# Expert stages with x parked in HBM, 21 instead of 14 up slabs beside the crossings, low parts behind the batches, and another order at the program's start

## What is computed

```python
def peer_ffn(x, w_q, sub_keys, u, v):
    q = (x @ w_q).reshape(B, S, PEER_HEADS, 2, hq)
    s_half = jnp.einsum('bshpc,hpkc->bshpk', q, sub_keys)
    top_s, top_i = lax.top_k(s_half, PEER_TOPK)
    ...
    best_s, best_pos = lax.top_k(cand_s.reshape(B, S, PEER_HEADS, n_cand), PEER_TOPK)
    experts = jnp.take_along_axis(...)
    gate = jax.nn.softmax(best_s, axis=-1)
    ...
        h = jax.nn.gelu(jnp.einsum('ted,td->te', u[ec], xc))
        return jnp.einsum('te,ted->td', gc * h, v[ec])
```

## Time and profile before

| | |
|---|---|
| runs | 4186.75 us median (4180.42 to 4187.92, 3 runs) |
| profiled execution | 4185.16 us, its span 4183.9 us |
| TensorE busy | 3972.6 us, 95% of the span; weight loads 92% |
| VectorE, ScalarE, GpSimd busy | 66%, 48%, 4% |
| mean granted clock | 0.975 of full speed |
| expert stage 0 | about 2335 to 3179 us; crossings 2574 to 2724 |
| expert stage 1 | about 3324 to 4166 us; crossings 3563 to 3717 |

### The profile page before, as it was taken

One profiled execution on the slowest core, in us unless ns is written; L12 is line 12 of the kernel. 1 busy time (PEld: TensorE's weight loads), 2 busy tenths in 40 slices (PEclk: granted clock), 3 DMA queues, 4 the chain that ended last, 5 costly groups with the idle time before them and its releaser, 6 DMA issues.

```text
span 4183.9 us, 78739 instructions
## 1 busy us (share of the span) xinstructions
PE 3972.6 (95%) x34162; PEld 3844.9 (92%) x34162; DVE 2741.8 (66%) x4076; ACT 1988.6 (48%) x2624; POOL 173.3 (4%) x212
## 2 busy tenths in 40 slices
PE   7989999999998999989989999899999999899999
PEld 7979999899996999979987899899998899899998
DVE  5566665665655657556545799844856699864765
ACT  4445444454443545454425545644444544654443
POOL 0011000110000000010013100000000000000000
PEclk9999999899999999999988999999999999999999
DMA  5534555345454455524541354455754355445754
GB/s 207 194 115 143 197 186 196 112 151 192 167 197 144 169 194 189 184 101 155 196 165 54 128 197 169 147 189 196 257 193 151 132 181 192 143 168 197 250 200 151
DMA packets 118633, 716.61 MB, mean 171 GB/s; under 512 B 13952, under 2 KB 19728, under 8 KB 37008
## 3 DMA queue, kind: packets, MB, share of 16 engines
q1 hardware_dynamic: 90864, 660.64, 44.7%
q10 hardware_dynamic: 26400, 43.28, 3.0%
q0 software_dynamic: 1024, 7.64, 0.5%
HBM read 690.38 MB, written 21.13 MB: 170 GB/s over the span
## 4 chain that ended last, share of the span: by engine, by line
PE 76%; DVE 12%; ACT 7%; issue 2%; DMA 2%; ACTq 1%; SPq 0%; DVEq 0%
PE psum L650 23%; PE psum L652 23%; PE psum L651 23%; DVE slab_low L1894 5%; ACT slab_high L1397 4%; PE psum L1040 1%; PE psum L1376 1%; DVE room L2541 1%; DMA peer_gates<-room 1%; DVE room L2520 1%; DVE h_parts L2177 1%; PE psum L1023 1%; ACT room L1808 1%; PE psum L1053 1%; ACT room L1645 1%
## 5 line engine op out<-in xcount | busy, mean ns | idle before, releaser
L1894 DVE TENSOR_TENSOR slab_low<-slab,slab_high 128x2048 fp32r<-128x2048 f32 x622 | 1424.9, 2291 | 880.9 <-ACT slab_high L1397 878.5
L650 PE MATMUL psum<-h_parts,slab_high 128*128 128x256 f32 x5632 | 1585.2, 281 | 56.5 <-DVE h_parts L2177 46.2
L1397 ACT ACTIVATE slab_high<-slab 128x2048 fp32r<-128x2048 f32 x630 | 1191.5, 1891 | 915.5 <-PE psum L652 798.4
L651 PE MATMUL psum<-h_parts,slab_high 128*128 128x256 f32 x5632 | 1564.2, 278 | 0.0
L652 PE MATMUL psum<-h_parts,slab_low 128*128 128x256 f32 x5632 | 1563.7, 278 | 0.0
L650 PEld LDWEIGHTS psum<-h_parts,slab_high 128*128 128x128 f32 x5632 | 1071.3, 190 | 78.0 <-issue 49.3
L650 PE MATMUL psum<-hidden_parts,slab_high 128*128 128x256 f32 x3840 | 1068.3, 278 | 26.5 <-DVE hidden_parts L2549 11.3
L651 PEld LDWEIGHTS psum<-h_parts,slab_high 128*128 128x128 f32 x5632 | 1071.8, 190 | 2.6 <-issue 2.4
L652 PEld LDWEIGHTS psum<-h_parts,slab_low 128*128 128x128 f32 x5632 | 1070.5, 190 | 0.0
L651 PE MATMUL psum<-hidden_parts,slab_high 128*128 128x256 f32 x3840 | 1062.0, 277 | 0.0
L652 PE MATMUL psum<-hidden_parts,slab_low 128*128 128x256 f32 x3840 | 1061.9, 277 | 0.0
(11 more groups left out here) (324 smaller groups left out, 3332.5 us busy)
## 6 DMA issues: line engine op xcount, KB each, us to landing
slab<-in_up SPq DMA_DIRECT2D x176, 1024.0 KB, 4.8
slab<-in_keys_up SPq DMA_DIRECT2D x128, 1024.0 KB, 4.8
slab<-in_keys_down SPq DMA_DIRECT2D x128, 1024.0 KB, 4.8
slab<-in_down SPq DMA_DIRECT2D x88, 1024.0 KB, 4.8
slab<-in_w_in SPq DMA_DIRECT2D x16, 1024.0 KB, 4.7
slab<-in_wq SPq DMA_DIRECT2D x16, 1024.0 KB, 4.8
peer_gates<-room ACTq DMA_DIRECT2D x64, 256.0 KB, 2.3
room<-peer_gates ACTq DMA_DIRECT2D x64, 256.0 KB, 4.6
```

The source lines that it names most:

```text
L650: nc.tensor.matmul(out, lhs[0], rhs[0], start=first, stop=False, **options)
L651: nc.tensor.matmul(out, lhs[0], rhs[1], start=False, stop=False, **options)
L1397: nc.scalar.activation(k.high[m % PARTS][:, 0:width], k.slabs[m % RING][:, 0:width], ACT.Copy).then_inc(k.rounded.up())
L1894: nc.vector.tensor_tensor(k.low[m % RING][:, 0:width], k.slabs[m % RING][:, 0:width], k.high[m % PARTS][:, 0:width], ALU.subtract).then_in ...
```

## The change

It does five things.

- **Room for hidden values.** The constants are sorted so that six (`LASTING`) come first. The others, and x, now lie at the bottom of the room. All stages but peer carve above them (`FLOOR`). peer carves its hidden rows from the very bottom: 32 + 21 up slabs fit.
- **x in HBM.** GpSimd stores x to `parked_x` after the squares, ScalarE waits for that before the first up is activated, and GpSimd loads x back once the 61st pair of hidden rows is split (`v.above_x` = 61); VectorE waits for it before the final adds.
- **EXTRA = 21.** The 32 batches lie in 38 windows, s = 2 to 39, beside 21 up slabs; then 11 downs alternate with the last 11 ups, 21 downs go beside the second multiplications, 32 behind. The number of slabs, matmuls, one-hots and gate transfers stays.
- **Low parts behind the batches.** In the crossings VectorE's `rest_slab` stands behind the step's batches.
- **Start and end.** Vectors load ahead of x, the constants wait until slab 1 is in. ScalarE and VectorE do six h chunks before slab 1; TensorE's second slab lags by 6 chunks (`FIRST_LAG`); the squares come last. x is stored in four pieces.

The diff, without the hunks that only move views above `FLOOR`:

```diff
--- before.py
+++ after.py
@@ -41,7 +41,7 @@
 NSEL = PH * TOPK
 ROUNDS = NKEYS // 2
 HALF = ROUNDS // 2
-EXTRA = 14
+EXTRA = 21
 BATCH = 8
 BATCHES = T // BATCH
 RETURNS = 6
@@ -106,13 +106,17 @@
     return {k: np.asarray(v, np.float32) for k, v in c.items()}
 
 
+LASTING = ("ident", "ones", "causal", "iota", "pick", "npick")
 CONST = constants()
+CONST = {k: CONST[k] for k in LASTING + tuple(k for k in CONST if k not in LASTING)}
 CONST_AT = {}
 _at = 0
 for _k, _v in CONST.items():
     CONST_AT[_k] = (_at, _v.shape[1], _v.shape[0])
     _at += _v.shape[1]
 CONST_W = _at
+LASTING_W = sum(CONST[k].shape[1] for k in LASTING)
+FLOOR = CONST_W - LASTING_W + DC * T
 
 
 VECTORS = [(f"ffn1_norm{l}", 8) for l in range(2)] + [(f"mix_norm{l}", 8) for l in range(2)] \
@@ -131,7 +135,7 @@
 
 RING = 4
 PARTS = 3
-AHEAD = 2
+FIRST_LAG = 6
 HIDDEN_W = FC * 2 * T
 RESIDUE = 240
 LEAD = RESIDUE % 32 // 4
@@ -192,19 +196,21 @@
         self.slabs = [sbuf(f"slab{i}", SLAB) for i in range(RING)]
         self.low = [sbuf(f"slab_low{i}", SLAB, F32R, place) for i, place in enumerate(places)]
         self.high = [sbuf(f"slab_high{i}", SLAB, F32R) for i in range(PARTS)]
-        self.x = sbuf("x", DC * T).rearrange("p (c t) -> p c t", t=T)
         at += (RESIDUE - 4 * LEAD - at) % 512
         self.h = sbuf("h_parts", LEAD + DC * 2 * T, F32R)[:, LEAD:].rearrange("p (c a t) -> p c a t", a=2, t=T)
         at = -(-at // 64) * 64
+        self.vectors = sbuf("vectors", VEC_W)
+        bottom = at + 4 * LASTING_W
         self.consts = sbuf("consts", CONST_W)
-        self.vectors = sbuf("vectors", VEC_W)
+        self.x = sbuf("x", DC * T).rearrange("p (c t) -> p c t", t=T)
+        assert at == bottom + 4 * FLOOR
 
         room_end = end - (end - RESIDUE) % 512
-        self.room_words = (room_end - at) // 4
+        self.room_words = (room_end - bottom) // 4
         self.early = sbuf("early_parts", LEAD + DC * 2 * T, F32R, at + (RESIDUE - 4 * LEAD - at) % 512)[:, LEAD:].rearrange("p (c a t) -> p c a t", a=2, t=T)
-        self.room = sbuf("room", self.room_words)
+        self.room = sbuf("room", self.room_words, alias=bottom)
         self.hidden = sbuf("hidden_parts", LEAD + HIDDEN_W, F32R, room_end - 4 * (LEAD + HIDDEN_W))[:, LEAD:].rearrange("p (c a t) -> p c a t", a=2, t=T)
-        self.taken = 0
+        self.taken = FLOOR
 
 
         self.arrived = [signal(f"slab_arrived{i}", 16) for i in range(RING)]
@@ -566,11 +573,11 @@
 def peer_views(k):
     v = Views()
 
+    k.taken = 0
     v.hidden = k.carve(2 * HALF + 2 * EXTRA, T)
     end = k.taken
-    k.taken = 0
     v.early = k.early
-    k.taken = DC * 2 * T + P
+    k.taken = FLOOR + DC * 2 * T + P
     v.h = k.carve(DC, T)
     v.square, v.squares, v.rstd, v.scales = k.carve(DC, T), k.carve(2, T), k.carve(T + TT), k.carve(TT)
     assert k.taken <= 2 * HALF * T
@@ -606,6 +613,7 @@
 
     late = HALF + EXTRA
     v.place = [2 * r if r < late else 2 * (r - late) for r in range(ROUNDS)]
+    v.above_x = late - (-FLOOR // (2 * T))
     windows = 2 * EXTRA - 4
     v.batches = [range(BATCHES * (s - 2) // windows, BATCHES * (s - 1) // windows) if 2 <= s < 2 + windows else range(0) for s in range(2 * EXTRA)]
     return v
@@ -695,13 +703,15 @@
                     nc.tensor.wait_ge(k.lines_copied.sem, 1)
             if f == 0:
 
-                firsts = [[part.rearrange("p (a k n) -> p a k n", a=2, k=DC) for part in self.take()] for _ in range(2)]
+                firsts, lag = [], FIRST_LAG if first else 2
                 pairs = [k.bank_pairs[g + k.first_pair][:, :, 0:T] for g in range(2)]
-                for step in range(DC + 2):
+                for step in range(DC + lag):
+                    if step in (0, lag):
+                        firsts.append([part.rearrange("p (a k n) -> p a k n", a=2, k=DC) for part in self.take()])
                     if step < DC:
                         nc.tensor.wait_ge(k.h_ready.sem, k.h_ready.at(step + 1))
                     for g in range(2):
-                        c = step - 2 * g
+                        c = step - lag * g
                         if not 0 <= c < DC:
                             continue
                         for a in range(2):
@@ -1428,6 +1438,10 @@
     def projected(self, n, by_token):
         return self.k.banks[n % 3].rearrange("p (a t) -> p a t", a=2)[:, :, 0:by_token or T]
 
+    def square_pair(self, v, j):
+        k, nc = self.k, self.k.nc
+        nc.scalar.activation(v.square[:, 2 * j:2 * j + 2, :], k.x[:, 2 * j:2 * j + 2, :], ACT.Square).then_inc(k.squared.up())
+
     def ffn(self, v, gain, first):
         k, nc = self.k, self.k.nc
         self.stage_enters(False)
@@ -1436,11 +1450,13 @@
         for c in range(DC):
             ready, value = k.x_ready(c // 2)
             nc.scalar.wait_ge(ready.sem, value)
+            if first and c == FIRST_LAG:
+                self.round_slab()
             nc.scalar.activation(k.h[:, c, 0, :], k.x[:, c, :], ACT.Copy, scale=k.vec(gain, c)).then_inc(k.h_rounded.up())
-            if c % 2 == 0:
-                continue
-            j = c // 2
-            nc.scalar.activation(v.square[:, 2 * j:2 * j + 2, :], k.x[:, 2 * j:2 * j + 2, :], ACT.Square).then_inc(k.squared.up())
+            if c % 2 and not first:
+                self.square_pair(v, c // 2)
+        for j in range(DC // 2 if first else 0):
+            self.square_pair(v, j)
         for tick in range(FC + 2):
             if tick < FC:
                 self.round_slab()
@@ -1756,6 +1772,7 @@
                     nc.scalar.wait_ge(k.scaled.sem, k.scaled.at(c + 1))
                     nc.scalar.activation(k.h[:, c, 0, :], v.h[:, c, :], ACT.Copy).then_inc(k.h_rounded.up())
         self.show_keys(v, PH - 1)
+        nc.scalar.wait_ge(k.parked.sem, k.parked.at(1))
         for r in range(HALF):
             self.round_slab()
             self.activate(v, r)
@@ -1929,9 +1946,10 @@
         nc.vector.wait_ge(k.h_rounded.sem, k.h_rounded.at(first + c + 1))
         nc.vector.tensor_tensor(k.h[:, c, 1, :], src, k.h[:, c, 0, :], ALU.subtract).then_inc(k.h_ready.up())
 
-    def add_down(self, slabs):
-
-        k, nc = self.k, self.k.nc
+    def add_down(self, slabs, parked=False):
+
+        k, nc = self.k, self.k.nc
+        back = k.unparked.at(1)
         pair_done, all_done = [k.pair_done.at(j + 1) for j in range(3)], k.slab_done.at(slabs)
 
         def finish(j):
@@ -1940,13 +1958,15 @@
                 nc.vector.wait_ge(k.pair_done.sem, pair_done[j])
             else:
                 nc.vector.wait_ge(k.slab_done.sem, all_done)
+            if parked and j == 0:
+                nc.vector.wait_ge(k.unparked.sem, back)
             nc.vector.tensor_tensor(both, k.banks[j].rearrange("p (a t) -> p a t", a=2), both, ALU.add).then_inc(k.x_done.sem)
         self.finish = finish
         k.x_done.later(DC // 2)
 
     def ffn(self, v, gain, first):
         k, nc = self.k, self.k.nc
-        self.early_input(k.vec(gain, 0, DC))
+        self.early_input(k.vec(gain, 0, DC), first=first)
         for tick in range(FC + 2):
             if tick < FC:
                 self.rest_slab()
@@ -2173,6 +2193,8 @@
         for c in range(DC):
             if c % 2 == 0 and c + 2 < DC:
                 self.finish(c // 2 + 1)
+            if first and c == FIRST_LAG:
+                self.rest_slab()
             nc.vector.wait_ge(k.h_rounded.sem, k.h_rounded.at(c + 1))
             nc.vector.scalar_tensor_tensor(out=parts[:, c, 1, :], in0=k.x[:, c, :], scalar=gains[:, c:c + 1], in1=parts[:, c, 0, :],
                                            op0=ALU.mult, op1=ALU.subtract).then_inc(k.h_ready.up())
@@ -2417,12 +2439,12 @@
         self.one_hots(v, 0)
         self.one_hots(v, 1)
         for s in range(2 * EXTRA):
-            if s % 2 == 0:
-                self.rest_slab()
             for b in v.batches[s]:
                 self.multiply(v, b)
                 if b + 2 < BATCHES:
                     self.one_hots(v, b + 2)
+            if s % 2 == 0:
+                self.rest_slab()
         self.separate(v, 0)
         for r in range(HALF - EXTRA):
             self.separate(v, r + 1)
@@ -2438,7 +2460,7 @@
             if r + 1 < ROUNDS:
                 self.separate(v, r + 1)
             self.rest_slab()
-        self.add_down(len(v.seq))
+        self.add_down(len(v.seq), parked=True)
 
     def top16(self, rows, values, where, n):
 
@@ -2652,8 +2674,12 @@
         self.add_squares(v)
 
     def peer(self, v):
+        k, nc = self.k, self.k.nc
         self.stage_enters(False)
         self.add_squares(v)
+        nc.gpsimd.dma_start(k.dram["parked_x"], k.x).then_inc(k.parked.up(), 16)
+        nc.gpsimd.wait_ge(k.hidden_ready.sem, k.hidden_ready.at(v.above_x))
+        nc.gpsimd.dma_start(k.x, k.dram["parked_x"]).then_inc(k.unparked.up(), 16)
 
 
 class SyncE:
@@ -2669,8 +2695,9 @@
 
     def store(self):
         k, nc = self.k, self.k.nc
-        nc.sync.wait_ge(k.x_done.sem, k.x_done.count)
```

(13 more changed lines are left out.)

9 lines of the change are left out of this document (5 added, 4 removed).

## The result

The changed kernel takes **4117.83 us** (median of 4 runs, 4110.86 to 4120.59), the kernel before beside it 4183.59 (4179.19 to 4187.92): ratio 0.984, 95% interval 0.9822 to 0.9859, 66 us faster. The profiled execution took 4120.59 us, its span 4118.9, 65.0 less than before. The prediction said 4135, and its range began at 4120: the direction and the places of the gain were right, its size was a fifth too small, and even its best sum, 4127, lay above the measured time.

The account below looks back on a forecast made before the run. TensorE, with work 95% of the span, was taken as the bound, VectorE being slower in the crossings; gains of 30.3 + 3.2 + 3.9 + 7.2 + 5 + 1.6 = 51.2 us from 4186.75 gave 4135, range 4120 to 4157.

Parts of the forecast that it names:

- Crossings: Expert stages: TensorE's 32.3 us of waits for one-hots go, 1 us a stage left; gain 30.3 us.
- First down: First down slab of each expert stage: waits of 4.4 and 3.0 us shrink to 2.1; gain 3.2 us.
- Second multiplications: Expert stages: the same 32 multiplications lie beside 21 slabs, waits of 1.9 and 2.0 us go; gain 3.9 us.
- Clock: Expert stages: TensorE's time at the lower clock mostly goes with the waits; gain 7.2 us, bounds 2 and 10.2.
- Start: Program start: h chunks begin earlier, so VectorE gets the square sum sooner; gain 5 us, bounds 1 and 7.
- End: Program end: x leaves in four pieces, three while VectorE still scales; gain 1.6 us.
- Parking: Expert stages: moving x to HBM and back costs nothing while the return stays below 21 us of cover.
- A wait in place of the one removed: Rival, crossings: three engines still wait for each other, half the crossing and clock gains stays; 4154 us, chance 0.12.
- Low parts late: Rival, 42 slabs: TensorE finds its next slab without low part, 1.7 us each; slower, 4207 us, chance 0.04.
- x comes back late: Rival, final adds: VectorE stands waiting for x, 13.2 us a stage, 26 us back; 4161 us, chance 0.05.
- terms 1 to 3: Expert stages: gains at the crossings, first down slab and second multiplications of 30.3, 3.2 and 3.9 us.
- term 4: Expert stages: the gain from TensorE's clock, one slow spell of 1.5 us a stage at most left; 7.2 us.

Follow-up runs that it names:

- e1: The changed kernel with EXTRA = 14 instead of 21, so the crossings lie beside 14 slabs as before: 4144.84 us.
- e2: The changed kernel with VectorE's low part ahead of the batches again, still 21 slabs beside the crossings: 4136.4 us.
- e3: The kernel before with one move, VectorE's low part behind the step's batches; 14 slabs, no parking, old start and end: 4153.99 us.
- e7: The changed kernel with bias table loaded and masked row written at the start, first crossing low part and first pair's rounding moved earlier: 4103.38 us.
- e6: The changed kernel with x brought back three pairs later, when the 64th pair is split and not the 61st: 4120.22 us.
- e9: The changed kernel with VectorE made slower in the crossings, four of eight one-hots of each second operand made twice: 4164.84 us.

## Why the prediction was too small

1. **Crossings** (30.3 forecast): recorded waits 32.3 before, 2.0 after, 1.0 a stage and at the first windows, as said. Right, but for the hidden part.
2. **First down** (2.1 left a stage): 2.0 and 2.0. The cause named, the rounding held up by a store, is what e1's ScalarE rows show. The size was the middle of two bounds, and that it fits so well is luck: the lower bound, 1.2, left out the last activation, which belongs to the chain.
3. **Second multiplications** (3.9): no wait left. Right.
4. **Clock** (7.2): 5.1 + 6.8 us lost before, 0.0 + 1.7 after: 10.2, the upper bound. "One slow spell of 1.5 us a stage at most, behind the first down's wait" came in one stage only; in e1, e2 and e3, where that wait is about 5 us, each stage has a spell twice as long there (3.4 us lost), and in e7 without the wait none.
5. **Start** (5): 4.9 at the square sum, 4.5 at the first stage's end. The number is right, the way to it in part luck: the 3.0 and 5.6 us were worked out for h chunks that begin at 11.5 and at 9.1 us, and 5 was chosen between. They began at 11.54, held by x, and the sum still came 4.9 earlier; slab 0 was rounded 3.3 us earlier (6.32 against 9.61), which the 3.0 had not counted. **End** (1.6): 1.9, from 13.5 to 11.6 us.
6. **Parking** (0): 0 in the expert stages, by e1 against e3. The cover was 24 us in stage 0, from the issue at 3122.96 to the adds at 3147.28, and 21.5 in stage 1 (21 forecast). The transfer took 5.8 and 5.6 us, where the prediction's estimate for this size was 4.4; the measured times decide. e6 shows that 5.1 us of cover just do.
7. **The rivals.** "A wait in place of the one removed" is out, since no such wait is left in the change; the margin was not 0.5 but about 0.7 us a slab (e9). "Low parts late" did not show: the one wait for slab_low is at the first window, where VectorE still waited for the slots. "x comes back late" took for granted that VectorE works without a pause where GpSimd issues; it pauses there for 1.1 us or more. So no run here tests the port rule of the Trainium skill ("SBUF — State Buffer", SBUF: two separate sides), by which a transfer issued by GpSimd is held up while VectorE holds the port they share.

**The step that failed is the size of a wait.** The recorded idle time of the expert stages fell by 19.1 + 18.9 = 38.0 us, where terms 1 to 3 gave 37.4. But the sum took a recorded wait as the whole of what it costs. The stages' length fell by 58.1: 38.0 idle, 10.2 clock, and 9.9 that no record calls idle, over 20 and 17 fewer gaps. With 0.25 us for each of 37 gaps the forecast would have been 9 lower, 4126, and with the whole clock (term 4 gave 7.2 of 10.2) 3 more, 4123. Most of the rest is in where it was counted from: the prediction started at a median of 4186.75, and in the set of runs beside the change the kernel before took 4183.59.
